# A two-block trunk kernel on one core: the second block's branch mix made from high and low fp32r parts, its weights in jobs of 128 columns, and the gate z moved ahead of the attention

## The chip, the cores and the metric

The kernel runs on one core of one Trainium2 chip. The metric is the device time of one execution in microseconds (us). Times of the kernel before: 4222.12, 4228.13 and 4229.13 us in three runs, median 4228.13 us.

## The reference, cut to what matters

Two transformer-like blocks follow one another on 1024 tokens of width 1024, all in float32. The change is in the second block, between its attention and its output projection:

```
h  = rms_norm(x, g_norm1) * (1 + sc1) + sh1           # 1024 tokens x 1024
hc = the same for 256 context tokens
aq, ak, av, dq, dk, dv, dz, da, db, ga, gd = split_cols(h @ w_in)
y_attn = window_ctx_attention(q_a, k_a, v_a, k_ac, v_ac, sink)      # 1024 x 512
o_dl   = gated delta rule over dq, dk, dv (both directions)         # 1024 x 512
y_d = rms_norm(o_dl, dn_norm_g) * silu(dz)                          # "gate z"
y   = sigmoid(ga) * (y_attn @ w_br_attn) + sigmoid(gd) * (y_d @ w_br_dn)   # branch mix
x   = x + gt1 * (y @ w_out)
x   = x + gt2 * mlp(x)                                              # 1024 -> 4096 -> 1024
```

`ga` and `gd` are 1024 wide, `w_br_attn` and `w_br_dn` are 512 x 1024. The branch mix is therefore two passes (attention, then delta rule) over 1024 x 1024 results, each result with a gate product of depth 1024 and a branch product of depth 512.

## The kernel before, in words

Every engine has an instruction stream of its own, written out by hand as a list of calls (`tensor`, `vector`, `scalar`, `gpsimd`, `sync`), and semaphores order them. Eight PSUM tiles of 128 x 512 are handed out in a ring by `Banks`: `open` takes the next one, `vacant` waits until the one eight places earlier has been emptied, `full` waits for a filled one. So an engine that empties a tile late holds TensorE up only when the ring comes round to that tile.

The stages of the second block, in TensorE's order, are: the delta rule; `qkv2` (queries, keys and values of the attention); `row` (the gain gt1 spread over the partitions); `watt`, the attention; `gated`, which makes y_d; `mix` with ps = 2 (attention branch) and ps = 3 (delta branch); `proj`, the output projection; and `ff`, the MLP.

`watt` runs over 64 units (8 query blocks x 8 heads). In its turn i TensorE makes the scores of unit i (L2281, local keys and context keys), turns the probabilities of unit i-3 (L2290) and multiplies those of unit i-4 with the values (L95). VectorE takes the scores out of PSUM (L2318, L2322), finds the maximum (L2325, L2327), makes the reciprocal for unit i-1 (L2333, L2335), and on every second turn copies a finished result out of PSUM (L2341, `tensor_copy` into `aq`). ScalarE makes the exponentials (L2352, L2353) and copies the turned probabilities of unit i-3 out of PSUM (L2362). GpSimd scales the probabilities (L2372). Scores live in 3 buffers, probabilities in 5, turned ones in 4.

`gated` makes z for 8 token tiles; for each, ScalarE a tanh, VectorE four operations (L2438 to L2446), and TensorE turns the result (L2397); ScalarE copies it to `yd` (L2413).

`mix` runs over 16 halves in a pass: 8 groups of 128 output columns, each for two halves of 512 tokens. A half has a gate product of 8 matmuls (tile "mg") and a branch product of 4 (tile "mo"), all float32, 128x128 weights by 128x512 tokens. ScalarE takes the tanh of "mg" (L837), VectorE multiplies with "mo" (L867), and in the second pass GpSimd adds the two branches (L896). The weights come as strips of 512 or 1024 columns, 2 MB each, into four fixed slots; SyncE issues each strip once a named product is through with the slot. The same functions serve the first block (ps = 0 and 1), which the change leaves as it is.

`ff` is written the other way. Each float32 operand is split into a high part that is rounded to fp32r, and a low part, the rest: ScalarE copies the weights to the high part (L1030), VectorE subtracts for the low part (L1037); activations likewise (L1099 and L1144). A product is then three fp32r matmuls: low x high, high x low, high x high. The weights of one job are 1 MB.

The normed tokens h of the second block lie in `HT`, are written to DRAM (`h_stash`) during the delta rule and read back before `qkv2`.

Of the kernel before, what the change touches and what calls it, by code (L numbers as in the profile page):

```python
# [130 lines left out]
def build(nc, d, out):  # L131
    ctx = ExitStack()
    with ctx:
# [12 lines left out]
        with nc.sbuf_tensor("below1", [P, 43008], F32), nc.sbuf_tensor("raw1", [P, 2048], F32) as RAW1, \  # L146
                nc.sbuf_tensor("between", [P, 3072], F32), nc.sbuf_tensor("turned", [P, 512], F32) as TMN:
            pass
        RR = ctx.enter_context(nc.sbuf_tensor("halves", [P, 52480], F32R))
# [53 lines left out]
        def strip_there(name):  # L203
            slot = STRIPS[name][0]
            k = 1 + [m for m in STRIPS if STRIPS[m][0] == slot].index(name)
            return l_w[slot].at(k + (1 if slot == BRA_SLOT and k >= BRA_NTH else 0))

# [25 lines left out]
            "bra": (0, None, 4, 1024, ("qkv", 7)),  # L233
            "g2a0": (1, w2[:, 2848:3360], 8, 512, ("kvv", 9)),
            "g2a1": (2, w2[:, 3360:3872], 8, 512, ("z", 7)),
            "brd": (3, d["w_br_dn_2"], 4, 1024, ("wp", 62)),
            "g2d0": (1, w2[:, 3872:4384], 8, 512, ("mg", 2, 0, 3, 1)),
            "g2d1": (2, w2[:, 4384:4896], 8, 512, ("mg", 2, 1, 3, 1)),
            "w20": (0, d["w_out_2"][:, 0:512], 8, 512, ("mo", 2, 1, 3, 1)),
            "w21": (3, d["w_out_2"][:, 512:1024], 8, 512, ("mo", 3, 1, 3, 1)),  # L240
        }
        BRA_SLOT = 0
        BRA_NTH = 1 + [m for m in STRIPS if STRIPS[m][0] == BRA_SLOT].index("bra")

        def sync_strip(e, name):
            slot, src, kt, n, after = STRIPS[name]
            if after is not None:
                e.wait_ge(*bk.full(after))
            view = strip_view(name)
            if name == "bra":  # L250
                for half in range(2):
                    e.dma_start(view[64 * half:64 * half + 64, :, :],
                                d["w_br_attn_2"][256 * half:256 * half + 256, :].rearrange(
                                    "(j f) n -> f j n", f=64)).then_inc(*l_w[slot].tick())
            else:
                e.dma_start(view, src.rearrange("(k p) n -> p k n", p=P)).then_inc(*l_w[slot].tick())
# [159 lines left out]
        def tensor_tm(e, st, key, t, N, emptied, c0=0):  # L416
# [5 lines left out]
            chain(e, o[:, 0:N], [(hlhs(k, t), w[:, k, c0:c0 + N]) for k in range(8)]).then_inc(*bk.filling(key))  # L422
# [318 lines left out]
        def vector_rec(e):  # L741
# [13 lines left out]
            for t in range(8):  # L755
# [22 lines left out]
        tmpy = [R(CB + i * 512, 512) for i in range(4)]  # L778
# [7 lines left out]
        yd = R3(F1, 4, 1024)  # L786
# [3 lines left out]
               (("ro0", "ro1"), ("gr0", "gr1"), 8, lambda k, n0, N: RC[:, k, n0:n0 + N], HB2, False),  # L790
               (("bra", "bra"), ("g2a0", "g2a1"), 4, lambda k, n0, N: aq[:, k, n0:n0 + N], None, True),
               (("brd", "brd"), ("g2d0", "g2d1"), 4, lambda k, n0, N: yd[:, k, n0:n0 + N], None, True)]
# [105 lines left out]

        o_ev, o_ad = C("proj_emptied_dve"), C("proj_added")
        G1 = R(CB + 2048, 1024)  # L900
# [19 lines left out]
        def vector_proj_tile(e, blk, c, t):  # L920
            key = ("wo", blk, c, t)
            dst = X[:, t, c * 512:(c + 1) * 512]
            i = c * 8 + t
            e.wait_ge(*bk.full(key))
            if blk == 0:
                e.scalar_tensor_tensor(out=dst, in0=bk.tile(key)[:, :], scalar=0.5, in1=dst, op0=ALU.mult,
                                       op1=ALU.add).then_inc(*bk.emptying(key))
            else:
                if i >= 4:
                    e.wait_ge(*o_ad.at(i - 3))  # L930
                elif i == 3:
                    e.wait_ge(*x_ad.at(32))
                e.scalar_tensor_tensor(out=tmpy[i % 4], in0=bk.tile(key)[:, :], scalar=0.5,
                                       in1=G1[:, c * 512:c * 512 + 512], op0=ALU.mult,
                                       op1=ALU.mult).then_inc(*bk.emptying(key))
# [32 lines left out]
        def gpsimd_proj(e):  # L968
            for c in range(2):
                for t in range(8):  # L970
                    dst = X[:, t, c * 512:(c + 1) * 512]
                    e.wait_ge(*bk.clear(("wo", 1, c, t)))
                    e.tensor_tensor(dst, dst, tmpy[(c * 8 + t) % 4], ALU.add).then_inc(*o_ad.tick())
# [577 lines left out]
        UNSPILL = [(0, 256), (256, 640), (640, 1280)]  # L1551
# [588 lines left out]
        wn = R(F0 + 8320, 384)  # L2140
        sk = R(F0 + 8704, 8)
# [9 lines left out]
        def tensor_qkv2(e):  # L2151
            for i in range(10 + 2):
                if i < 10:
                    for c0 in (c0 for c0, c1 in UNSPILL if c0 // 128 == i):
                        e.wait_ge(*l_unspill[c0].at(1))
                    if i < 8:
                        tensor_tm(e, "aq", ("qkv", i), i, 512, k_ea)
                    tensor_tm(e, "akv", ("kvv", i), i, 256, k_ea)
# [95 lines left out]
        sc_ = [R(T1 + i * 640, 640) for i in range(3)]  # L2254
        pp_ = [R(T1 + 1920 + i * 640, 640) for i in range(5)]
        pT_ = [R3(T1 + 5120 + i * 640, 5, 128) for i in range(4)]
# [49 lines left out]

        def vector_watt(e):
            e.wait_ge(*l_wn.at(1))
            e.wait_ge(*l_sk.at(1))
            for i in range(64 + 4):  # L2310
# [26 lines left out]
                if 0 <= u < 64 and u % 2:  # L2337
# [3 lines left out]
                    e.tensor_copy(aq[:, j, n * 128:(n + 1) * 128], bk.tile(key)[:, 0:128]).then_inc(*bk.emptying(key))  # L2341

        def scalar_watt(e):
            for i in range(64 + 3):
# [11 lines left out]
                if 0 <= u < 64:  # L2356
                    if u >= 4:
                        e.wait_ge(*bk.full(("wp", (u - 4) - (u - 4) % 2)))
                    for c0, n4 in watt_quads(u):
# [4 lines left out]
                                     ACT.Copy).then_inc(*bk.emptying(key))  # L2364

# [19 lines left out]
        def tensor_gated(e):  # L2385
            for i in range(9):
                if i < 8:
                    tensor_tm(e, "z", ("z", i), i, 512, y_ev)
# [87 lines left out]
        l_x2, l_x3, l_out = LD("x2"), LD("x3"), LD("out")  # L2476
        x_of = lambda src: src.rearrange("(t p) n -> p t n", p=P)

        def tensor(e):
# [18 lines left out]
            tensor_row(e, 0, TM1)  # L2498
            tensor_watt(e)
            tensor_gated(e)  # L2500
            for ps in (2, 3):
                if ps == 2:
                    e.wait_ge(*bk.clear(("wp", 62)))
                else:
                    e.wait_ge(*bk.clear(("zt", 7)))
                tensor_mix(e, ps)
# [3 lines left out]
        def vector(e):  # L2510
# [27 lines left out]
            vector_row(e, 16, TM1)  # L2538
            vector_watt(e)
            vector_gated(e)  # L2540
            vector_mix(e, 2)
            vector_mix(e, 3)
# [4 lines left out]
        def scalar(e):  # L2547
# [21 lines left out]
            scalar_gated_root(e)  # L2569
            scalar_watt(e)  # L2570
            scalar_gated(e)
            scalar_mix(e, 2)
            scalar_mix(e, 3)
# [3 lines left out]
        def gpsimd(e):  # L2577
# [16 lines left out]
            e.wait_ge(*y_z.at(8))  # L2594
            gpsimd_mix(e, 3)
            e.wait_ge(*l_x3.at(1))
# [3 lines left out]
        def sync(e):  # L2600
# [47 lines left out]
            for c0, c1 in UNSPILL:  # L2648
                if c0:
                    e.wait_ge(*e_o.at(16))  # L2650
                e.dma_start(HT[:, :, c0:c1], h3[:, :, c0:c1]).then_inc(*l_unspill[c0].tick())
# [103 lines left out]
```

## Time and profile before

| what | value |
| --- | --- |
| median of the runs | 4228.13 us (4222.12 to 4229.13) |
| the profiled execution | 4222.77 us, of which the profile's span is 4220.9 us |
| mean granted TensorE clock | 0.969 of full speed |
| TensorE busy (PE) | 4017.8 us, 95% of the span |
| VectorE (DVE) / ScalarE (ACT) / GpSimd (POOL) busy | 1733.0 / 1014.7 / 691.2 us |
| DMA | 211.36 MB, mean 50 GB/s |

PE is TensorE's matmul, PEld its weight load, which overlaps it. Times in the trace are counted from the start of the span. A float32 matmul stands in the trace as two records. Some matmul records are missing from the trace, so the period of the work is better read from the engine that empties PSUM than from a count of matmuls.

### The profile page before, as it was taken

To read this page: it belongs to the slowest core of one execution; us is meant where nothing else is said; L and a number is where in the kernel's file an instruction comes from. 1 tells how busy PE (TensorE), PEld (TensorE's weight loads), DVE (VectorE), ACT (ScalarE), POOL (GpSimd) and SP (SyncE) were. 2 spreads that over 40 slices of the span, in tenths; PEclk is the share of its full clock that TensorE was granted. 3 is DMA by queue.
4 is the path that set the end of the run, shared out by engine and by line. 5 is a ranking of instruction groups with operands and counts; after the bars stand their busy time and mean duration, and the time that the engine had idled before them with its cause. 6 is when DMAs were issued, how large, how long until landed. Compare 5 with 4: busy or idle time off the path is not lost. (4 is left out here: it accounts for less than half of the span.)

```text
span 4220.9 us, 41996 instructions
## 1 busy us (share of the span) xinstructions
PE 4017.8 (95%) x16528; PEld 2670.7 (63%) x16528; DVE 1733.0 (41%) x3083; ACT 1014.7 (24%) x1757; POOL 691.2 (16%) x533
## 2 busy tenths in 40 slices
PE   8988999999999999999988998979999998999998
PEld 4465444444468888887546888657544447888886
DVE  2165776532132332234557895477300023322232
ACT  1044553000032112213433322145200012112210
POOL 1053000000001001101011110035100112333333
PEclk9999999999999999998998997989999999999999
DMA  3200102333011111122002121210102001111111
GB/s 143 58 1 3 44 4 70 110 110 130 30 40 50 50 50 50 49 78 113 1 5 42 30 41 43 96 37 1 40 20 80 8 23 60 50 50 40 50 50 50
DMA packets 179089, 211.36 MB, mean 50 GB/s; under 512 B 63952, under 2 KB 125008, under 8 KB 178512
## 3 DMA queue, kind: packets, MB, share of 16 engines
q1 hardware_dynamic: 119536, 172.50, 12.2%
q10 hardware_dynamic: 59360, 36.19, 3.2%
q8 instruction: 134, 2.20, 0.2%
q14 instruction: 59, 0.48, 0.0%
HBM read 185.33 MB, written 21.50 MB: 49 GB/s over the span
## 5 line engine op out<-in xcount | busy, mean ns | idle before, releaser
L95 PE MATMUL ps<-arena 128*128 128x512 f32 (+4 forms) x5360 | 1915.1, 514 | 53.1 <-DVE arena L550 25.2
L95 PEld LDWEIGHTS ps<-arena 128*128 128x128 f32 (+1 forms) x5360 | 934.6, 189 | 970.1 <-issue 911.3
L95 PE MATMUL ps<-halves 128*128 128x512 f32 x6144 | 1401.4, 390 | 20.9 <-DVE halves L388 11.0
L95 PEld LDWEIGHTS ps<-halves 128*128 128x128 f32 x6144 | 1157.0, 188 | 263.9 <-DVE halves L388 11.2
L1144 DVE TENSOR_TENSOR halves<-tmps,halves 128x512 fp32r<-128x512 f32 x128 | 88.6, 692 | 524.0 <-ACT halves L1099 524.0
L1123 POOL TENSOR_TENSOR tmps<-tmps 128x512 f32<-128x512 f32 x128 | 137.4, 1074 | 999.8 <-ACT tmps L1091 999.8
L867 DVE SCALAR_TENSOR_TENSOR arena<-arena,ps 128x512 f32<-128x512 f32 x64 | 43.8, 686 | 507.4 <-PE ps L95 507.3
L1030 ACT ACTIVATE halves<-raws 128x2048 fp32r<-128x2048 f32 x62 | 118.4, 1910 | 555.5 <-PE ps L95 524.6
L896 POOL TENSOR_TENSOR arena<-arena 128x512 f32<-128x512 f32 x32 | 41.5, 1297 | 1067.2 <-DVE arena L867 1067.2
L1130 POOL TENSOR_TENSOR arena<-arena 128x512 f32<-128x512 f32 x128 | 164.6, 1293 | 191.5 <-DVE arena L1167 191.5
L1037 DVE TENSOR_TENSOR halves<-raws,halves 128x2048 fp32r<-128x2048 f32 x62 | 142.1, 2292 | 73.6 <-ACT halves L1030 73.6
L1167 DVE TENSOR_TENSOR arena<-ps,arena 128x512 f32<-128x512 f32 x128 | 87.8, 690 | 194.9 <-PE ps L95 188.7
L1091 ACT ACTIVATE tmps<-ps 128x512 f32<-128x512 f32 x128 | 76.5, 598 | 376.6 <-PE ps L95 376.6
L1159 DVE TENSOR_TENSOR arena<-arena,ps 128x512 f32<-128x512 f32 x128 | 87.2, 686 | 187.8 <-PE ps L95 187.8
L574 POOL TENSOR_SCALAR arena<-arena,sm 128x512 f32<-128x512 f32 x64 | 100.0, 1562 | 238.2 <-DVE sm L543 238.2
L1649 POOL TENSOR_TENSOR arena<-arena 128x512 f32<-128x512 f32 x40 | 49.5, 1261 | 512.1 <-PE ps L95 261.3
L2372 POOL TENSOR_SCALAR arena<-arena,wst 128x640 f32<-128x640 f32 (+1 forms) x64 | 115.3, 1803 | 104.5 <-DVE wst L2335 104.5
L886 DVE SCALAR_TENSOR_TENSOR arena<-arena,sc 128x256 f32<-128x256 f32 x224 | 117.4, 524 | 8.0
L1099 ACT ACTIVATE halves<-tmps 128x512 fp32r<-128x512 f32 x128 | 81.1, 634 | 149.2 <-POOL tmps L1123 149.2
L837 ACT ACTIVATE arena<-ps,hb 128x512 f32<-128x512 f32 x32 | 21.9, 686 | 387.4 <-PE ps L95 387.4
L1755 DVE TENSOR_TENSOR arena<-arena 64x30 f32<-64x30 f32 (+5 forms) x300 | 102.0, 340 | 13.2 <-ACT arena L1453 3.2
L1758 DVE TENSOR_TENSOR arena<-arena 64x30 f32<-64x30 f32 (+5 forms) x300 | 102.1, 340 | 10.3
(262 smaller groups left out, 3218.5 us busy)
## 6 DMA issues: line engine op xcount, KB each, us to landing
arena<-in_w_in SPq DMA_DIRECT2D x20, 2048.0 KB, 8.6
raws<-in_w_ff SPq DMA_DIRECT2D x31, 1024.0 KB, 5.4
raws<-in_w_mlp SPq DMA_DIRECT2D x31, 1024.0 KB, 5.2
arena<-in_w_ada ACTq DMA_DIRECT2D x24, 1024.0 KB, 5.2
arena<-in_w_out SPq DMA_DIRECT2D x4, 2048.0 KB, 13.8
h_stash<-arena SPq DMA_DIRECT2D x1, 5120.0 KB, 21.3
inverses<-arena ACTq DMA_DIRECT2D x20, 256.0 KB, 2.9
arena<-in_x SPq DMA_DIRECT2D x4, 1024.0 KB, 10.6
```

The lines of the kernel that those rows point to most:

```text
L95: ins = e.matmul(out_ap, l, r, start=i == 0, stop=i == n - 1)
L574: e.tensor_scalar(pbuf[i % 4], pbuf[i % 4], c[:, 2:3], None, ALU.mult).then_inc(*a_sl.tick())
L886: e.scalar_tensor_tensor(out=a, in0=raw_a[:, kk, :], scalar=sc3[:, kk, b:b + 1], in1=a, op0=ALU.mult, op1=ALU.add).then_inc(*(m_part if kk ...
L1030: e.activation(RR[:, FW + q * 4096:FW + q * 4096 + 2048], raw_of(n), ACT.Copy).then_inc(*f_wh.tick())
L1037: e.tensor_tensor(RR[:, FW + q * 4096 + 2048:FW + q * 4096 + 4096], raw_of(n), RR[:, FW + q * 4096:FW + q * 4096 + 2048].bitcast(F32), ALU ...
L1123: e.tensor_tensor(tt, tt, tt, ALU.mult).then_inc(*f_sq.tick())
L1130: e.tensor_tensor(dst, dst, tmg[(i * 8 + t) % 2], ALU.add).then_inc(*f_ad.tick())
L1144: e.tensor_tensor(fl[:, m, n0:n0 + N], ftmp[x % 2], fh[:, m, n0:n0 + N].bitcast(F32), ALU.subtract).then_inc(*f_fl.tick())
L1167: e.tensor_tensor(tmg[x % 2], bk.tile(key)[:, :], G2[:, nh * 512:nh * 512 + 512], ALU.mult).then_inc(*bk.emptying(key))
L1755: e.tensor_tensor(T3, bc(W3[:, k:k + 1, k + 1:32], [64, k, 31 - k]), bc(W3[:, 0:k, k:k + 1], [64, k, 31 - k]), ALU.mult).then_inc(*dv.tick())
L1758: e.tensor_tensor(W3[:, 0:k, k + 1:32], W3[:, 0:k, k + 1:32], T3, ALU.add).then_inc(*(i_sol if k == 30 else dv).tick())
L2372: e.tensor_scalar(p[:, 0:nl + 256], p[:, 0:nl + 256], wst[:, i % 8, 3:4], None, ALU.mult).then_inc(*w_sl.tick())
```

## The change

1. `mix` for ps = 2, 3 is replaced by `mix2`. Each product of depth 8 or 4 is three fp32r matmuls per depth step, as in `ff`. The weights of one group of 128 columns (8 gate and 4 branch tiles, 768 KB) are one job; 16 jobs, two raw buffers. ScalarE rounds the 128x1536 weights to the high part, VectorE subtracts for the low part.
2. The tokens are split into high and low parts during `watt`: at turns 6, 9, ..., 51 ScalarE makes a 128x512 high part and VectorE, at the end of the same turn, the low part (16 pieces). The attention's result is split as it leaves PSUM: the copy writes the high part, and a second VectorE instruction, behind a wait for the first, the low part (32 of them).
3. y_d is split during the first pass of `mix2` (8 pieces of 128x512).
4. `gated` comes ahead of `watt` on TensorE, VectorE and ScalarE.
5. The tokens are read back into other buffers (`HT2`, `HC`) in seven transfers, where there were three; x is read back in two halves, one during the second pass and one after it; and the projection's first strip is loaded when job 14 is through, its second at the end of the mix.

```diff
+        def sync_mix2(e, j):
+            ps, c, m = JOBS2[j]
+            c0 = c * 512 + m * 128
+            if j >= 2:
+                e.wait_ge(*bk.full(("mo",) + JOBS2[j - 2] + (1,)))
+            else:
+                e.wait_ge(*bk.full(("kvv", 9)))
...
+            e.dma_start(raw[:, 0:8, :], w2[:, g0:g0 + 128].rearrange("(k p) n -> p k n", p=P)).then_inc(*ld.tick())
...
+        def scalar_mix2_weights(e, j):
...
+            e.wait_ge(*weights2_there(j))
+            if j >= 2:
+                e.wait_ge(*bk.full(("mo",) + JOBS2[j - 2] + (1,)))
+            e.activation(RR[:, o + 1536:o + 3072], MW2[j % 2][:, :], ACT.Copy).then_inc(*m2_hi.tick())
+        def vector_mix2_weights(e, j):
...
+            e.wait_ge(*m2_hi.at(j + 1))
+            e.tensor_tensor(RR[:, o:o + 1536], MW2[j % 2][:, :], RR[:, o + 1536:o + 3072].bitcast(F32),
+                            ALU.subtract).then_inc(*m2_lo.tick())
+        def three(e, o, lefts, rights):
+            prods = []
+            for (lh, ll), (rh, rl) in zip(lefts, rights):
+                prods += [(ll, rh), (lh, rl), (lh, rh)]
+            return chain(e, o, prods)
+        def tensor_mix2(e, ps):
+            for i, (c, m, h) in enumerate(MIXED):
...
+                key = ("mg", ps, c, m, h)
+                o = bk.open(key, x_ea)
+                e.wait_ge(*bk.vacant(key))
+                e.wait_ge(*m2_lo.at(j + 1))
+                if j == 0:
+                    e.wait_ge(*h_lo.at(8 * (h + 1)))
+                three(e, o[:, :], W[0:8], [(H2H[k][:, n0:n0 + 512], H2L[k][:, n0:n0 + 512]) for k in range(8)]
+                      ).then_inc(*bk.filling(key))
...
+        def scalar_mix2(e, ps):
+            for i, (c, m, h) in enumerate(MIXED):
+                u = (ps % 2) * 16 + i
+                if h == 0:
+                    scalar_mix2_weights(e, (ps - 2) * 8 + i // 2 + 1)
...
+        def vector_mix2(e, ps):
+            for i, (c, m, h) in enumerate(MIXED):
...
+                if h == 0:
+                    vector_mix2_weights(e, (ps - 2) * 8 + i // 2 + 1)
...
-        UNSPILL = [(0, 256), (256, 640), (640, 1280)]
+        UNSPILL = [(0, 256), (256, 640), (640, 1024), (1024, 1280)]
...
+        SPLIT_AT = {6 + 3 * x: (x % 8, x // 8) for x in range(16)}
+        def scalar_tokens_hi(e, kk, h):
...
+            e.activation(H2H[kk][:, cols], HT2[kk // 4][:, kk % 4, cols], ACT.Copy).then_inc(*h_hi.tick())
+        def vector_tokens_lo(e, kk, h):
...
+            e.wait_ge(*h_hi.at(h_lo.n + 1))
+            e.tensor_tensor(H2L[kk][:, cols], HT2[kk // 4][:, kk % 4, cols], H2H[kk][:, cols].bitcast(F32),
+                            ALU.subtract).then_inc(*h_lo.tick())
...
@@ vector_watt, every second turn, and at the end of the turns in SPLIT_AT
-                    e.tensor_copy(aq[:, j, n * 128:(n + 1) * 128], bk.tile(key)[:, 0:128]).then_inc(*bk.emptying(key))
+                    e.tensor_copy(AQH[:, j, cols], bk.tile(key)[:, 0:128]).then_inc(*dv.tick())
+                    e.wait_ge(*dv.now())
+                    e.tensor_tensor(AQL[:, j, cols], bk.tile(key)[:, 0:128], AQH[:, j, cols].bitcast(F32),
+                                    ALU.subtract).then_inc(*bk.emptying(key))
+                if i in SPLIT_AT:
+                    vector_tokens_lo(e, *SPLIT_AT[i])
@@ scalar_watt, at the end of the turn, behind the copies of unit i-3
+                if i in SPLIT_AT:
+                    scalar_tokens_hi(e, *SPLIT_AT[i])
@@ the order on TensorE (VectorE and ScalarE likewise)
             tensor_row(e, 0, TM1)
+            tensor_gated(e)
             tensor_watt(e)
-            tensor_gated(e)
             for ps in (2, 3):
-                if ps == 2:
-                    e.wait_ge(*bk.clear(("wp", 62)))
-                else:
-                    e.wait_ge(*bk.clear(("zt", 7)))
-                tensor_mix(e, ps)
+                tensor_mix2(e, ps)
@@ the order on VectorE, behind vector_watt
+            vector_mix2_weights(e, 0)
+            vector_mix2(e, 2)
+            vector_mix2(e, 3)
@@ the SyncE queue
-            for st in ("bra", "g2a0", "brd", "g2a1", "g2d0", "g2d1"):
-                sync_strip(e, st)
-            e.wait_ge(*bk.full(("mo", 2, 1, 3, 1)))
-            e.wait_ge(*l_stash.at(1))
-            e.dma_start(X, x_of(xs)).then_inc(*l_x3.tick())
-            for st in ("w20", "w21"):
-                sync_strip(e, st)
+            for j in range(16):
+                sync_mix2(e, j)
+                if j == 10:
+                    e.wait_ge(*l_stash.at(1))
+                    e.dma_start(X[:, 0:4, :], x_of(xs)[:, 0:4, :]).then_inc(*l_x3[0].tick())
+            sync_strip(e, "w20")
+            e.wait_ge(*bk.full(("mo", 3, 1, 3, 1)))
+            e.dma_start(X[:, 4:8, :], x_of(xs)[:, 4:8, :]).then_inc(*l_x3[1].tick())
+            sync_strip(e, "w21")
```

## Rows read from the trace of the kernel before

**Rows 1.** The page's first part: busy time, share of the span, instructions.
```profile
PE 4017.8 (95%) x16528; PEld 2670.7 (63%) x16528; DVE 1733.0 (41%) x3083; ACT 1014.7 (24%) x1757; POOL 691.2 (16%) x533
```

**Rows 2.** Windows over attention, mix, MLP: length, busy by engine, granted clock, DMA.
```profile
2776.00:2978.00 202.00, 196.93 (x1155) 139.82 (x1154) 143.03 (x415) 109.18 (x307) 115.34 (x64) 0.97 0.00 1
...
3041.70:3379.70 338.00, 338.00 (x785) 149.37 (x785) 21.95 (x32) 19.70 (x33) 20.20 (x16) 0.99 0.11 40
...
3526.00:4150.00 624.00, 624.00 (x2753) 516.49 (x2752) 182.52 (x200) 127.00 (x148) 207.06 (x171) 1.00 0.15 48
```

**Rows 3.** Timeline of ScalarE in the mix: start, us, engine, line, idle before.
```profile
3060.58 0.60 ACT L837 ACTIVATE arena<-ps 128x512 f32<-128x512 f32 x1 [9.70 <-PE ps L95]
3070.88 0.60 ACT L837 ACTIVATE arena<-ps 128x512 f32<-128x512 f32 x1 [9.70 <-PE ps L95]
```

**Rows 4.** Timeline of ScalarE in the MLP, one entry for each 24 fp32r matmuls.
```profile
3799.06 0.60 ACT L1091 ACTIVATE tmps<-ps 128x512 f32<-128x512 f32 x1 [3.06 <-PE ps L95]
...
3804.50 0.60 ACT L1091 ACTIVATE tmps<-ps 128x512 f32<-128x512 f32 x1 [3.06 <-PE ps L95]
```

**Rows 5.** The page's groups by line: the splitting instructions of the MLP.
```profile
L1144 DVE TENSOR_TENSOR halves<-tmps,halves 128x512 fp32r<-128x512 f32 x128 | 88.6, 692 | 524.0 <-ACT halves L1099 524.0
...
L1030 ACT ACTIVATE halves<-raws 128x2048 fp32r<-128x2048 f32 x62 | 118.4, 1910 | 555.5 <-PE ps L95 524.6
...
L1037 DVE TENSOR_TENSOR halves<-raws,halves 128x2048 fp32r<-128x2048 f32 x62 | 142.1, 2292 | 73.6 <-ACT halves L1030 73.6
...
L1099 ACT ACTIVATE halves<-tmps 128x512 fp32r<-128x512 f32 x128 | 81.1, 634 | 149.2 <-POOL tmps L1123 149.2
```

**Rows 6.** Timeline of one turn of the attention and the start of the next.
```profile
2900.19 0.56 DVE L2318 SCALAR_TENSOR_TENSOR arena<-ps,arena 128x384 f32<-128x384 f32 x1 [0.55 <-PE ps L2281]
...
2901.97 0.21 DVE L2327 TENSOR_SCALAR wst<-wst,arena 128x1 f32<-128x1 f32 x1
...
2902.22 0.29 ACT L2352 ACTIVATE wst<-arena,wst 128x1 f32<-128x1 f32 x1 [1.45 <-DVE wst L2327]
2902.28 0.16 DVE L2335 RECIPROCAL wst<-wst 128x1 f32<-128x1 f32 x1
2902.42 0.81 ACT L2353 ACTIVATE arena<-arena,wst 128x640 f32<-128x640 f32 x1
...
2902.45 1.34 PE L2281 MATMUL ps<-arena 64*128 64x384 f32 x4
2902.54 1.88 POOL L2372 TENSOR_SCALAR arena<-arena,wst 128x640 f32<-128x640 f32 x1 [1.32 <-DVE wst L2335]
...
2903.23 0.74 ACT L2362 ACTIVATE arena<-ps 128x512 f32<-128x512 f32 x2
2903.39 0.56 DVE L2318 SCALAR_TENSOR_TENSOR arena<-ps,arena 128x384 f32<-128x384 f32 x1 [0.95 <-PE ps L2281]
...
2903.72 0.76 PE L2290 MATMUL ps<-identm,arena 128*128 128x128 f32 x5
...
2905.76 0.29 DVE L2341 COPY arena<-ps 128x128 f32<-128x128 f32 x1
```

**Rows 7.** Timeline: the attention's last instructions, and the last of the gate.
```profile
2977.87 0.60 ACT L2362 ACTIVATE arena<-ps 128x512 f32<-128x512 f32 x1 [1.01 <-PE ps L2290]
...
2979.65 0.29 DVE L2341 COPY arena<-ps 128x128 f32<-128x128 f32 x1 [2.13 <-PE ps L95]
...
3041.72 0.60 ACT L2413 ACTIVATE arena<-ps 128x512 f32<-128x512 f32 x1 [3.22 <-PE ps L2397]
```

**Rows 8.** DMA issues of the whole span: KB each, median us to landing.
```profile
raws<-in_w_mlp SPq DMA_DIRECT2D x31, 1024.0 KB, 5.2
...
arena<-in_w_out SPq DMA_DIRECT2D x4, 2048.0 KB, 13.8
```

**Rows 9.** Timeline of the projection: one VectorE and one GpSimd instruction that overlap.
```profile
3428.56 2.28 DVE L1037 TENSOR_TENSOR halves<-raws,halves 128x2048 fp32r<-128x2048 f32 x1
...
3428.72 3.24 POOL L973 TENSOR_TENSOR arena<-arena 128x512 f32<-128x512 f32 x1 [5.61 <-DVE arena L933]
```

More of the change, by code:

```diff
@@ L205, in strip_there @@
             k = 1 + [m for m in STRIPS if STRIPS[m][0] == slot].index(name)
-            return l_w[slot].at(k + (1 if slot == BRA_SLOT and k >= BRA_NTH else 0))
+            return l_w[slot].at(k)
         SLOTS = [W0, W0 + 4096, W0 + 8192, F0 + 12288]
@@ L249, in sync_strip @@
             view = strip_view(name)
[L250 to L254, printed above, removed]
-            else:
-                e.dma_start(view, src.rearrange("(k p) n -> p k n", p=P)).then_inc(*l_w[slot].tick())
+            e.dma_start(view, src.rearrange("(k p) n -> p k n", p=P)).then_inc(*l_w[slot].tick())
         hrhs = lambda k, n0, N: HT[:, k, n0:n0 + N]
@@ L421, in tensor_tm @@
             e.wait_ge(*strip_there(st))
-            chain(e, o[:, 0:N], [(hlhs(k, t), w[:, k, c0:c0 + N]) for k in range(8)]).then_inc(*bk.filling(key))
+            chain(e, o[:, 0:N], [(tokens(k, t), w[:, k, c0:c0 + N]) for k in range(8)]).then_inc(*bk.filling(key))
         def tensor_qkv(e):
@@ new lines, in build, with weights2_there, weights2 @@
+        l_m = [LD("mix_weights0"), LD("mix_weights1")]
+        m2_hi, m2_lo = C("mix_weights_hi"), C("mix_weights_lo")
+        yd_hi, yd_lo = C("gated_hi"), C("gated_lo")
+        parts2 = lambda j: 3 if j < 8 else 2
+        def weights2_there(j):
+            return l_m[j % 2].at(sum(parts2(x) for x in range(j % 2, j + 1, 2)))
+        def weights2(j, part, k):
+            o = PL2[j % 2] + (1536 if part == "hi" else 0) + k * 128
+            return RR[:, o:o + 128]
+        YDH = [RR[:, o:o + 512] for o in [26624 + 512 * i for i in range(5)] + [37376 + 512 * i for i in range(3)]]
@@ new lines, in three @@
+        def three(e, o, lefts, rights):
[5 more added lines that the diff above has]
+            for i, (c, m, h) in enumerate(MIXED):
+                j = (ps - 2) * 8 + i // 2
+                n0 = h * 512
+                W = [(weights2(j, "hi", k), weights2(j, "lo", k)) for k in range(12)]
+                key = ("mg", ps, c, m, h)
[6 more added lines that the diff above has]
+                      ).then_inc(*bk.filling(key))
+                key = ("mo", ps, c, m, h)
+                o = bk.open(key, x_ev)
+                e.wait_ge(*bk.vacant(key))
+                if ps == 2:
+                    e.wait_ge(*bk.clear(("wp", 62)))
+                    right = [(AQH[:, k, n0:n0 + 512], AQL[:, k, n0:n0 + 512]) for k in range(4)]
+                else:
+                    e.wait_ge(*yd_lo.at(8))
+                    right = [(YDH[2 * k + h], YDL[2 * k + h]) for k in range(4)]
+                three(e, o[:, :], W[8:12], right).then_inc(*bk.filling(key))
@@ L2473, in build @@
         TM1, TM2 = R3(Z2 + 1024, 8, 128), R3(47104, 8, 128)
[L2476 removed]
+        l_x2, l_out = LD("x2"), LD("out")
         x_of = lambda src: src.rearrange("(t p) n -> p t n", p=P)
```

134 lines of the change are left out of this document (94 added, 40 removed).

## The prediction

> **What bounds the kernel now.** I read the page first: TensorE is busy for 95% of the span, every other engine for less than half of it [rows 1]. So time is won or lost where TensorE's own work gets shorter or where it is made to wait. Then the windows of the stages that the change touches [rows 2]. In the mix TensorE is busy for all of the 338 us, while VectorE, ScalarE and GpSimd work about 20 us each: that stage is TensorE's work and nothing else, and its neighbours have room. In the attention TensorE is busy for 197 of 202 us, but here VectorE has 143 us of work, ScalarE 109 and GpSimd 115; the room is small, and what is added lands in a chain. The MLP, already written in high and low parts, keeps TensorE busy for all of its 624 us at a granted clock of 1.00, that is 2.4 GHz, so the new form can be fed. Last I read the timelines for periods.
>
> **The products.** In the mix ScalarE's tanh comes once per half, 3060.58 and then 3070.88: 10.30 us for 12 float32 products of 128x128 by 128x512 [rows 3], 0.86 us each. In the MLP one relu follows another at 3799.06 and 3804.50: 5.44 us for 24 fp32r matmuls [rows 4], 0.227 us each. A half of the new mix has 12 x 3 = 36 of these, 8.16 us. There are 32 halves: 32 x (10.30 - 8.16) = **68.5 us less**. The price of one matmul is well known, since shapes and operand types are those of the MLP, so this term has an error of about 1 us.
>
> **The weights.** A job is two halves, 16.3 us. Its split costs ScalarE 1910 ns x 1536/2048 = 1.43 us and VectorE 2292 ns x 1536/2048 = 1.72 us [rows 5]. The load for job j+1 is issued when job j begins. It must land, be rounded and be subtracted before job j+1: 16.3 - 1.43 - 1.72 - about 0.2 for semaphores leaves 12.9 us for the transfer. The trace has no transfer of 768 KB in rows of 512 bytes. By bytes, a 1024 KB load lands in 5.2 us [rows 8], which makes 3.9 us; by rows (this load has 1536 of 512 bytes, the other 1024 of 1 KB) 7.8 us. The longer end still leaves 5 us, so I take nothing. While ScalarE waits for the load it holds up the tanh, and VectorE behind it the multiply, but the ring of eight tiles covers two jobs. The y_d pieces (0.63 and 0.69 us each, eight times) go into halves of 8.16 us: nothing. The first projection strip is 2 MB, asked for 16.3 us before the projection, and lands in 13.8 us [rows 8]: nothing, with 2 us to spare. x and the second strip are needed some 30 and 55 us into the projection: nothing.
>
> **The attention.** This is where a cost falls. A turn takes 3.20 us (2900.19 to 2903.39), and VectorE's own part ends at 2902.44; it then sits idle 0.95 us until the next scores are there [rows 6]. So it could do a turn in 2.2 us. Two things are added.
> The second instruction at the copy out of PSUM: 0.29 us for the copy [rows 6], as much again for the subtraction and some 0.1 us of waiting between, 0.65 us together with the copy, on every second turn.
> The token pieces, on every third turn. VectorE's low part stands at the end of its turn, and waits for ScalarE's high part of the same turn, which stands behind ScalarE's exponentials and its copies. In the times of rows 6: the maximum is out at 2902.18, ScalarE's exponentials run until 2903.23, its two copies until 2903.97, the high part (0.63, rows 5) until 2904.60, then VectorE's low part (0.69) until 2905.35 [rows 5, 6]. Such a turn is 5.15 us long for VectorE, 2.2 of it spent waiting, with the next unit's scores, maximum and reciprocal queued behind it. It must make that good in the two following turns. Over six turns (two with pieces, four without, three copies of which one hides in a wait): 2 x 5.15 + 4 x 2.2 + 2 x 0.65 = 20.4 us. TensorE needs 6 x 3.20 = 19.2 us. VectorE becomes the bound by 1.2 us per six turns, 7.5 times between turns 9 and 53: 9 us. The PSUM ring adds a little: the tile that the subtraction frees is wanted again within the next turn of TensorE, and following the turns with this rule gives 1.6 in place of 1.2, that is 12 us. I take **10 us more**. Below, it could be nothing, if ScalarE reaches its copies earlier than drawn and the three score buffers smooth the rest; above, see the rivals.
>
> **The port.** GpSimd's scaling begins at 2902.54, right behind the reciprocal, and ends at 2904.42 [rows 6]; the low part would begin at 2904.65, so by the rows they miss one another by 0.2 us. That they would disturb one another is seen elsewhere: an addition of GpSimd that began 0.16 us into a VectorE subtraction with two SBUF inputs took 3.24 us where its neighbours take 1.26 [rows 9]. The Trainium skill's page "SBUF — State Buffer", section "Who interferes with whom", states this as a rule: a VectorE instruction with two SBUF inputs and a GpSimd instruction that reads SBUF share a read port, and the later one waits for the whole of the other. The trace agrees, in that one addition. By the rows' order the sum stays at 10 us for the attention; by the rule, were the 16 low parts each to meet a scaling, it would be the rival with the port below.
>
> **The seam behind the attention.** Before, the gate's first product starts at once. Now TensorE's first mix product waits for the weights of job 0, which VectorE splits after its last attention instruction. ScalarE's last copy ends at 2978.47, the rounding at 2979.90. VectorE's last copy runs from 2979.65 to 2979.94 [rows 7], its new subtraction ends at 2980.3, the weights' low part 1.72 us later, at 2982.0. TensorE is done at 2979.6. It waits 2.5 us and a semaphore: **2.6 us more**, between 1 and 4.
>
> **The gate moved.** The same instructions run in another place. Its last turn costs TensorE the same wait, 3.22 us in the trace [rows 7], since ScalarE and VectorE must finish tile 7 before it can be turned. Its strip and its row of gains are loaded long before. VectorE's sums of squares and the row product still come first on their queues. I take nothing. The one thing that can differ is TensorE's clock at the attention's start. The attention's window has a mean granted clock of 0.97 against 1.00 in the MLP [rows 2]: 3% of 202 us, 6 us, is all that a low clock costs there. It could go (6 us less) or double (6 us more); the idle stretches that bring it are the same, so zero.
>
> **The sum.** -68.5 + 10 + 2.6 = -55.9 us. The profiled execution took 4222.77 us, its span and 1.9 us around it; it would become 4166.9. The median of the runs lies 5.4 us above that execution, so the median forecast is 4228.1 - 55.9 = **4172 us**.
>
> **Rivals.**
> *The attention isn't slowed.* For it: the average load of VectorE stays under 3.2 us per turn if the wait for ScalarE were not there, and three score buffers give slack. Against it: VectorE is the engine that waits, and a wait of 2.2 us is longer than the 0.95 us it has spare. Then 68.5 - 2.6 = 65.9 us less: 4162.
> *The port.* For it: the gap of 0.2 us is small, and when VectorE runs late the phases move. Against it: the scaling is released by VectorE's own reciprocal, which always stands just ahead of the wait. If each of the 16 low parts waited for one scaling of 1.88 us [rows 6], 30 us come on top: 4202. Half of it gives 4187. A TensorE that idles more and is granted a lower clock goes the same way.
> *The weights come late: slower than before.* One mechanism: the load of a job in rows of 512 bytes, at the start of each job's period. If landing takes L, a period is L + 1.43 + 1.72 + 0.2, and 15 periods follow the first job. All of the gain is gone when 16.3 + 15 x period = 329.6 - 12.6, at a period of 20.05 us, that is L = 16.7 us. At L = 20 the mix takes 367 us and the kernel 4278. The nearest rows say 5.2 us for a larger load [rows 8], three times less than needed. A slower end for the first strip (13.8 us) is also under it.
>
> **How the numbers follow.** The forecast has 0.60, with a range of its own of 4164 to 4184. The attention not slowed 0.18. The port, or any other loss of over 15 us in the attention, 0.18. The late weights 0.03, and 0.01 for a no-change by a mixture. 0.2% is 8.5 us, about what a measurement of this kernel can tell from no change; all cases but the last two are beyond it on the fast side: faster 0.96, same 0.01, slower 0.03. The range goes from 4158 (the unslowed attention with a few us of clock won back) to 4190 (half of the port's price): it leaves out about 0.15, most of it above.
>
> **What the profile after would show.** The tanh of the mix every 8.16 us, TensorE busy throughout the mix, VectorE some 50 us of work in it. If the tanh is at more, the products or the weights are the failed step; waits of TensorE for VectorE's weight subtraction, once a job, would name the weights. In the attention: VectorE idle for some 2 us ahead of each of 16 subtractions, released by ScalarE; TensorE idle ahead of its scores or transposes, released by VectorE; the stage some 10 us longer than 202. If GpSimd's scaling or the subtraction has a maximum far above 1.88 and 0.69 us, it is the port. Behind the attention one TensorE wait of 2.6 us. The gate some 62 us long, with one wait of 3.2 us. The forecast is wrong above all if the attention's growth is not 10 us; next, if the transfers take over 13 us.

## The result, and the profile after

| | before | changed |
| --- | --- | --- |
| median of 4 runs | 4226.39 us (4222.12 to 4229.13) | 4190.49 us (4187.09 to 4196.68) |
| span of the profiled execution | 4220.9 us | 4185.3 us |
| mean granted TensorE clock | 0.969 | 0.964 |

The ratio is 0.9918, 95% interval 0.99 to 0.9935: faster by 36 us. The forecast was 56 us less, 4172, with a range of 4158 to 4190, so the direction was right, the size was not, and the time lies just outside the range.

The mix first. ScalarE's timeline, changed kernel:

```profile
3237.09 0.60 ACT L998 ACTIVATE arena<-ps 128x512 f32<-128x512 f32 x1 [6.65 <-PE ps L95]
3244.76 1.49 ACT L942 ACTIVATE halves<-mixw 128x1536 fp32r<-128x1536 f32 x1 [7.08 <-DMA mixw<-in_w_br_dn]
3246.16 0.58 ACT L998 ACTIVATE arena<-ps 128x512 f32<-128x512 f32 x1
3253.41 0.60 ACT L998 ACTIVATE arena<-ps 128x512 f32<-128x512 f32 x1 [6.67 <-PE ps L95]
```

The tanh of a job's second half comes at 3237.09 and 3253.41, 16.32 us apart: 8.16 for a half, where it was 10.30 [rows 3]. The tanh of the first half is late, since ScalarE stands 7.08 us for the weights' transfer; that costs nothing. The windows of the attention (its first scores to its last product) and of the mix:

```profile
2839.26:3073.91 234.65, 215.14 (x1169) 151.78 (x1168) 160.31 (x462) 118.10 (x322) 115.50 (x64) 0.91 0.00 1
...
3076.30:3337.30 261.00, 260.97 (x1151) 216.21 (x1152) 51.39 (x54) 42.54 (x54) 19.38 (x15) 1.00 0.21 59
```

TensorE is busy throughout the mix. The attention is the surprise. In the kernel before, the same stretch was:

```profile
2775.50:2979.60 204.10, 199.03 (x1170) 141.71 (x1169) 143.03 (x415) 110.00 (x307) 115.34 (x64) 0.97 0.00 1
```

It grew by 30.6 us, where 10 were forecast. TensorE's idle time in it went from 5.1 to 19.5 us, and its busy time, with the same matmuls, from 199.0 to 215.1, at a granted clock of 0.91 in place of 0.97.

The whole difference of the spans, from the stages' ends in both timelines (each to some 0.2 us, by the instruction taken as the end): everything up to the gate +1.3; the gate +0.3; the attention +30.6; the seam behind it +2.4; the mix -69.9; all behind it -0.3. Together -35.6 us.

One late turn in the timeline of the changed kernel (weight loads and GpSimd left out):

```profile
2923.76 0.21 DVE L2464 TENSOR_SCALAR wst<-wst,arena 128x1 f32<-128x1 f32 x1
...
2924.21 0.81 ACT L2496 ACTIVATE arena<-arena,wst 128x640 f32<-128x640 f32 x1
...
2925.02 0.74 ACT L2505 ACTIVATE arena<-ps 128x512 f32<-128x512 f32 x2
...
2925.66 0.62 ACT L2436 ACTIVATE halves<-tokens 128x512 fp32r<-128x512 f32 x1
...
2926.31 0.69 DVE L2441 TENSOR_TENSOR halves<-tokens,halves 128x512 fp32r<-128x512 f32 x1 [2.07 <-ACT halves L2436]
2926.92 0.55 DVE L2455 SCALAR_TENSOR_TENSOR arena<-ps,arena 128x384 f32<-128x384 f32 x1
...
2928.70 0.21 DVE L2464 TENSOR_SCALAR wst<-wst,arena 128x1 f32<-128x1 f32 x1
...
2929.14 0.81 ACT L2496 ACTIVATE arena<-arena,wst 128x640 f32<-128x640 f32 x1
...
2929.74 0.33 PE L2413 MATMUL ps<-identm,arena 128*128 128x128 f32 x1 [0.37 <-DVE halves L2481]
...
2929.96 0.74 ACT L2505 ACTIVATE arena<-ps 128x512 f32<-128x512 f32 x2
...
2930.84 2.15 PE L95 MATMUL ps<-arena 128*64 128x128 f32 x10 [0.77 <-ACT arena L2505]
```

VectorE waits 2.07 us for ScalarE's high part, where 2.2 were forecast. Its next maximum is out 4.94 us after the last one (2923.76 to 2928.70), so ScalarE's next exponentials and, behind them, its copies of turned probabilities are late, and TensorE's product with the values waits for those copies, 0.77 us here. Just before, TensorE's last transpose also waited 0.37 us for the second instruction at the copy (L2481), which holds a tile of the ring. Up to the attention's last turns the first of these waits is the large one, by the view of TensorE's waits (us in total, times, longest); the kernel before has none of either there:

```profile
PE ps L95 <- ACT arena L2505: 12.2, 12, 1.6
PE ps L2413 <- DVE halves L2481: 2.6, 7, 0.4
```

After the waits of this turn the granted clock falls; windows of 5 us:

```profile
2926.00:2931.00 5.00, 3.85 (x24) 2.52 (x23) 4.52 (x12) 2.03 (x6) 1.96 (x2) 1.00 0.00 0
2931.00:2936.00 5.00, 5.00 (x17) 3.41 (x16) 1.85 (x7) 1.75 (x5) 2.04 (x2) 0.51 0.02 5
```

0.51 is the lower level, 1.2 GHz. There are five such falls in the middle of the attention; the kernel before has a low clock at the attention's start, and none later. At the lower level TensorE takes longer for a turn, and behind four of the five falls it doesn't wait when VectorE is late the next time: of VectorE's 16 late turns it waits for 12, 14.8 us in all.

### The profile page after: what moved, and what is told of

The parts are those of the page before. It is cut to its first block and busy times, and to the rows that moved or that the text cites. A ratio compares the mean times of both kernels' runs of the same rounds, so it can differ in the third digit from the quotient of the medians.

```text
span 4185.3 us, 42926 instructions
## 1 busy us (share of the span) xinstructions
PE 3963.6 (95%) x16912; PEld 2751.7 (66%) x16912; DVE 1783.1 (43%) x3155; ACT 1049.6 (25%) x1797; POOL 692.6 (17%) x533
## 5 line engine op out<-in xcount | busy, mean ns | idle before, releaser
L95 PE MATMUL ps<-halves 128*128 128x512 f32 x7296 | 1665.0, 391 | 23.3 <-DVE halves L378 11.0
L95 PEld LDWEIGHTS ps<-halves 128*128 128x128 f32 x7296 | 1374.7, 189 | 312.2 <-issue 11.4
L95 PE MATMUL ps<-arena 128*128 128x512 f32 (+4 forms) x4208 | 1448.2, 501 | 65.2 <-DVE arena L544 25.0
L95 PEld LDWEIGHTS ps<-arena 128*128 128x128 f32 (+1 forms) x4208 | 721.9, 190 | 736.2 <-issue 667.4
L95 PE MATMUL ps<-arena,tokens 128*128 128x512 f32 (+1 forms) x384 | 140.0, 522 | 0.0
L830 ACT ACTIVATE arena<-ps,hb 128x512 f32<-128x512 f32 x32 | 21.9, 686 | 389.9 <-PE ps L95 389.9
L95 PEld LDWEIGHTS ps<-arena,tokens 128*128 128x128 f32 x384 | 72.3, 191 | 62.1 <-issue 59.1
L860 DVE SCALAR_TENSOR_TENSOR arena<-arena,ps 128x512 f32<-128x512 f32 x32 | 21.9, 687 | 202.4 <-PE ps L95 202.4
```

Source lines behind the costliest of these rows:

```text
L95: ins = e.matmul(out_ap, l, r, start=i == 0, stop=i == n - 1)
```

## The experiments

Three theories. **A, the wait:** VectorE's wait for ScalarE makes it late, and TensorE has no lead to absorb it. **B, the work:** VectorE's added instructions, or their meeting with GpSimd at a shared port. **C, the ring:** the second instruction at the copy out of PSUM. The attention's length is read for each as above, from the first scores to the last product with the values.

**1. The low part one turn later.** In `vector_watt`:

```diff
-                if i in SPLIT_AT:
-                    vector_tokens_lo(e, *SPLIT_AT[i])
+                if i - 1 in SPLIT_AT:
+                    vector_tokens_lo(e, *SPLIT_AT[i - 1])
```

> The low part of each token piece is made by VectorE at the end of the turn after the one in which ScalarE makes its high part; nothing else is changed. Theory A (the wait: VectorE stands 1.4 to 2.1 us in its own turn for ScalarE's high part, and TensorE has only some 0.3 us of lead, so the lateness passes on to it): the wait is gone, the attention falls from 234.6 us to between 205 and 212 (before: 204.1), its granted clock from 0.91 back to 0.97, and the kernel lands near 4160 to 4167. Theory B (VectorE's added work of 17 us itself, or the port that it shares with GpSimd): the attention stays at 228 us or more. Theory C (the second instruction at the copy out of PSUM, which holds a tile of the ring): it stays at 228 or more.

Measured: the attention 207.6 us; the kernel 4160.64 us, ratio to the kernel before 0.9852 (0.982 to 0.9885). Theory A's number; B and C fall.

**2. The high part first.** In `scalar_watt`, the same work on both engines, in the same turn:

```diff
+                    if i in SPLIT_AT:
+                        scalar_tokens_hi(e, *SPLIT_AT[i])
                     e.wait_ge(*w_mx.at(i + 1))
...
-                if i in SPLIT_AT:
-                    scalar_tokens_hi(e, *SPLIT_AT[i])
```

> ScalarE makes the high part of a token piece at the start of its turn, ahead of the exponentials, while it waits for the maximum anyway; VectorE's low part stays at the end of the same turn. VectorE then begins it right behind its reciprocal, just as GpSimd begins to scale. Theory A: no wait of VectorE for ScalarE ahead of the low part, the attention at 205 to 213 us. Theory B, by the port: the low part or the scaling next to it takes 0.6 to 1.9 us longer in each of 16 turns, and the attention stays at 225 us or more. Theory C: 228 or more.

Measured: one run of 4159.61 us, the attention 203.3:

```profile
2842.94:3046.26 203.32, 198.26 (x1169) 141.26 (x1168) 162.00 (x462) 118.02 (x322) 118.23 (x64) 0.98 0.00 1
```

VectorE has as much work in it as in the changed kernel (162.0 against 160.3 us), and the stage is 31 us shorter. As for the port, all 16 low parts now overlap a scaling of GpSimd, and they do so in two orders, eight times each:

```profile
2975.41 0.67 DVE L2441 TENSOR_TENSOR halves<-tokens,halves 128x512 fp32r<-128x512 f32 x1
2975.59 2.25 POOL L2517 TENSOR_SCALAR arena<-arena,wst 128x640 f32<-128x640 f32 x1 [1.32 <-DVE wst L2472]
...
2985.20 1.88 POOL L2517 TENSOR_SCALAR arena<-arena,wst 128x640 f32<-128x640 f32 x1 [1.32 <-DVE wst L2472]
2985.74 0.79 DVE L2441 TENSOR_TENSOR halves<-tokens,halves 128x512 fp32r<-128x512 f32 x1
```

Alone, as in the changed kernel, the low part takes 0.69 us and the scaling 1.88. Where the low part begins 0.18 us ahead, the scaling takes some 0.36 us longer; where it begins 0.34 to 0.55 us behind, the low part takes 0.79 us (once 1.00), and the scaling nothing more. No low part waits for a whole scaling. What is left of it on the path is at most the 0.5 us by which this attention is longer than that of run 4 below.

**3. Without the second instruction at the copy.** The branch product of the first pass takes the high part twice; the low part of the attention's result is left out of the computation.

```diff
-                    e.tensor_copy(AQH[:, j, cols], bk.tile(key)[:, 0:128]).then_inc(*dv.tick())
-                    e.wait_ge(*dv.now())
-                    e.tensor_tensor(AQL[:, j, cols], bk.tile(key)[:, 0:128], AQH[:, j, cols].bitcast(F32),
-                                    ALU.subtract).then_inc(*bk.emptying(key))
+                    e.tensor_copy(AQH[:, j, cols], bk.tile(key)[:, 0:128]).then_inc(*bk.emptying(key))
```

> The second VectorE instruction at the copy out of PSUM is left out, and the branch product of the first pass uses the high part in its place (the low part of the attention's result is left out of the computation). Theory A: the attention falls only by what 32 instructions of 0.3 us take from the catching up, to between 225 and 234 us, and the waits for ScalarE stay. Theory C: the attention falls to 215 us or less.

Measured: one run of 4190.39 us, the attention 232.7. C falls: TensorE's 2.6 us of waits for L2481 are gone, and those for ScalarE's copies take their place, 15.7 us in place of 12.2.

**4. All pieces behind the attention.**

```diff
             vector_watt(e)
+            for x in SPLIT_AT.values():
+                vector_tokens_lo(e, *x)
             vector_mix2_weights(e, 0)
```

(and ScalarE's high parts likewise; none inside.)

> All 16 token pieces are split behind the attention, so none is in it. Theories A and B: the attention at 205 to 208 us, and TensorE waits behind it for 16 low parts and the weights, some 13 us in place of 2.4; the kernel near 4170. Theory C: the attention stays at 225 us or more, since the second instruction at the copy is still in it. Beside e1 it tells A from B: if e1 is as fast in the attention as e4, the work of the 16 low parts costs nothing there and only the wait did.

Measured: one run of 4172.99 us, the attention 202.8, TensorE's wait behind it 12.05. Beside run 2 with its 203.3: sixteen low parts in the attention cost 0.5 us there, once nothing waits. The work is nearly free, and the wait was the price.

**5. The seam.** As run 2, with the weights of job 0 rounded in turn 60 and subtracted in turn 64.

```diff
+                if i == 60:
+                    scalar_mix2_weights(e, 0)
                 u = i - 3
...
                     e.reciprocal(c[:, 3:4], c[:, 1:2]).then_inc(*w_rc.tick())
+                if i == 64:
+                    vector_mix2_weights(e, 0)
```

> As the run with the high part first, and the weights of job 0 are rounded by ScalarE in turn 60 of the attention and subtracted by VectorE in turn 64, where it waits for TensorE anyway. Theory A with the seam as costed: the attention stays at 203 us, TensorE's wait of 2.4 us behind it goes, the kernel some 2 us faster than the one with the high part first: near 4157, about 0.983 to 0.985 of the kernel before. If the wait stays at 2.4 us, something else than the weights releases the first mix product.

Measured: 4159.26 us (4154.75 to 4165.43), ratio 0.9846 (0.983 to 0.9862). TensorE's wait behind the attention, 2.42 us in the changed kernel and in run 2, is gone: the product begins as the attention ends. The attention was 209.3 us here, against 203.3: not by waits, its idle time is 6.9 us, but by its start, where the clock stayed low some 9 us longer. The kernel's time doesn't show the 2 us.

**6. Half of the waits.** As run 2, but at even turns the high part stays at the end of the turn.

> Pieces at odd turns have their high part first, pieces at even turns keep it at the end of the turn, so VectorE waits in 8 turns in place of 16. Theory A: the cost goes with the number of waits, the attention at some 219 us (half way between 203 and 235). If the granted clock falls only when idle stretches follow one another closely, it stays at 0.97 and the attention is at 212 to 216, since the idle part alone is 14 us for 16 waits.

```profile
2846.47:3061.07 214.60, 200.31 (x1169) 141.65 (x1168) 160.40 (x462) 118.08 (x322) 115.50 (x64) 0.98 0.00 1
```

Measured: one run of 4176.48 us, the attention 214.6, at a clock of 0.98. Eight waits cost (214.6 - 203.3) / 8 = 1.4 us each, 1.15 of it idle time (14.3 against 5.1 us in all), and the clock didn't fall in the middle. Sixteen at this price make 22.6 us, 225.9; the changed kernel has 234.7. The other 9 us are what its falls of the clock cost on balance: its busy time is 16 us above the kernel before, but a slower TensorE waits less. So the cost has two parts. With half of the waits the second didn't come; what brings it is not shown.

**7 and 8. VectorE late by work.** As run 2, with one or three more subtractions per piece into unused places.

```diff
             e.wait_ge(*h_hi.at(h_lo.n + 1))
+            for r in range(1):   # 3 in the second
+                e.tensor_tensor(RR[:, (3072, 3584, 7168)[r]:(3584, 4096, 7680)[r]], HT2[kk // 4][:, kk % 4, cols],
+                                H2H[kk][:, cols].bitcast(F32), ALU.subtract).then_inc(*dv.tick())
+            e.wait_ge(*dv.now())
```

> High part first, and VectorE does one more subtraction of the same size per piece, into an unused place (16 more of 0.69 us; the result is not used). VectorE's part of such a turn grows from 2.9 to 3.6 us, or 4.2 with the copy, against TensorE's 3.2 and its lead of 0.3. Theory A (what counts is VectorE's lateness beyond that lead, whatever its reason): 0.1 us in half of the turns and 0.7 in the others, the attention at 207 to 212 us. If TensorE could run ahead by a turn or more, as the forecast had it, the two following turns would take it up and the attention would stay at 203 to 205.

> As the last, with three more subtractions per piece: VectorE's part of such a turn is some 5.0 us, near the 5.15 us of the change, but filled with work and with no wait for ScalarE. Theory A: as late, so as slow: the attention at 228 to 240 us, and the granted clock near 0.91. If it is ScalarE's wait itself that matters and not VectorE's lateness, the attention stays below 220.

Measured: one more, 4171.84 us and an attention of 216.5; three more, 4221.81 us and 271.0, at clocks of 0.96 and 0.78:

```profile
2842.05:3058.56 216.51, 203.02 (x1169) 143.87 (x1168) 174.14 (x478) 118.11 (x322) 118.41 (x64) 0.96 0.00 1
```

```profile
2837.30:3108.30 271.00, 249.99 (x1169) 176.05 (x1168) 196.46 (x510) 118.09 (x322) 122.54 (x64) 0.78 0.00 1
```

Both are above what was expected. With one more, the idle time grew by 8.4 us (13.5 against 5.1), where lateness beyond the lead was expected to cost 8 x 0.1 + 8 x 0.7 = 6.4; the other 4.8 us are busy time, from a low clock at the start. With three more VectorE is as late as in the changed kernel or a little later, since the copy out of PSUM no longer hides in a wait and GpSimd's scaling runs beside the subtractions (up to 2.77 us where it takes 1.88). Idle time is 21.0 us, close to the changed kernel's 19.5. But TensorE's busy time is 250.0 us in place of 215.1, all by the clock. That lateness by work costs what lateness by waiting costs holds for the idle part; how far the clock falls was not foreseen.

**9. TensorE's idle stretches filled.** As run 5, with three float32 matmuls each ahead of the last gate tile and of the first transposes; their results are overwritten.

```diff
+                        if u == 0:
+                            for _ in range(3):
+                                e.matmul(o[:, :], ak[:, 0:128], ak[:, 0:512], start=True, stop=True)
                         e.wait_ge(*w_sl.at(u + 1))
```

> As the run with the high part first and the weights of job 0 early. In addition TensorE does three float32 matmuls of 128x128 by 128x512 (0.86 us each at the full clock) whose result is overwritten, at two places where it sits idle: ahead of the last gate tile (3.2 us idle) and ahead of the attention's first transposes (3.6 us idle). If the idle stretches are what brings the clock down at the attention's start, its first 16 us are no longer at 0.5 to 0.7 and the attention falls from 203 to 209 us to some 197 to 200, the kernel by 4 to 8 us. If the clock falls anyway, the fillers run at half speed and cost a few us instead.

```profile
2841.00:2846.00 5.00, 3.67 (x13) 1.66 (x11) 4.72 (x16) 2.68 (x8) 3.05 (x2) 1.00 0.00 0
2846.00:2851.00 5.00, 3.90 (x16) 2.82 (x16) 2.52 (x10) 2.96 (x8) 3.21 (x3) 0.71 0.00 2
2851.00:2856.00 5.00, 5.00 (x21) 3.62 (x20) 2.86 (x9) 2.00 (x5) 1.56 (x1) 0.61 0.01 3
```

Measured: 4154.71 us (4151.42 to 4162.62), ratio 0.9837 (0.9823 to 0.985); the attention 205.5 us. The clock stays up through the filled stretches and falls at about 2848 all the same, behind small waits (0.25 to 1.30 us) in the first turns. It stays low for 7 us, where run 5's profile has two low stretches of some 4 and 17 us. The expected 4 to 8 us aren't shown: the median is 4.6 us lower, but the interval overlaps that of run 5.

**10. TensorE given a lead.** The changed kernel with all its waits; only the product with the values, and the copy out of PSUM, come one turn later.

```diff
 tensor_watt, vector_watt
-            for i in range(64 + 4):
+            for i in range(64 + 5):
...
-                u = i - 4
+                u = i - 5
 scalar_watt
-                    if u >= 4:
-                        e.wait_ge(*bk.full(("wp", (u - 4) - (u - 4) % 2)))
+                    if u >= 5:
+                        e.wait_ge(*bk.full(("wp", (u - 5) - (u - 5) % 2)))
 five buffers of turned probabilities: pT_[u % 4] -> pT_[u % 5]
```

> The changed kernel with its waits as they are; only TensorE's product of the probabilities with the values runs one turn later (unit i-5 in turn i, five buffers of turned probabilities), and the copy out of PSUM with it. Theory A in full: what left TensorE only 0.3 us of lead is that this product waits for ScalarE's copies, which stand behind the exponentials of the newest unit. With a turn more, TensorE takes up most of VectorE's late turns, and only VectorE's own load (20.4 us in six turns by the forecast's sum, against 19.2) is left: the attention at 208 to 218 us in place of 234.6, the clock near 0.97, all 16 waits of VectorE still there. If another link holds TensorE (the ring of PSUM tiles), the attention stays at 225 us or more.

```profile
2843.11:3055.98 212.87, 203.97 (x1169) 144.18 (x1168) 158.56 (x462) 118.19 (x323) 115.34 (x64) 0.95 0.00 1
```

```profile
DVE halves L2441 <- ACT halves L2436: 26.1, 16, 2.1
```

Measured: one run of 4169.82 us, the attention 212.9. The second fence is the waits' view: all 16 waits of VectorE for ScalarE are there, 26.1 us of them, where the same view has 13, of 21.9 us, for the changed kernel. The attention is 9 us longer than before and not 31, and TensorE's waits for ScalarE's copies, 12.2 us in the changed kernel, are gone. This was the link. (VectorE's copy out of PSUM moved with the product, and its waits for that product went from 12.1 to 5.5 us; the run doesn't tell the two halves of the loop apart.)

Of the 8.8 us, 3.8 are idle time and 4.9 busy time. The clock was low somewhat longer at the start, and fell once later, for some 7 us, right behind one single wait:

```profile
2877.02 1.97 PE L95 MATMUL ps<-arena 128*64 128x128 f32 x8 [1.41 <-DVE halves L2481]
```

## Why the prediction was wrong, and where it was right

**Right: the products.** 8.16 us per half was forecast and measured. The mix gave 69.9 us, where 68.5 were forecast. The rest is of the size of what the kernel before lost at the start of its mix, where the granted clock was low (0.72 and 0.94 in the two windows of 5 us from 3040); the new mix is at 1.00 throughout.

**Right: the weights.** The transfer asked for as a job began let the rounding start 4.7 to 6.4 us later, in the median 5.0, between the two bounds of 3.9 and 7.8. The rounding took 1.49 us (1.43 forecast), the subtraction 1.76 (1.72). TensorE never waited for them within the mix.

**Right: the seam,** 2.42 us for 2.6, and run 5 shows its cause. **Right: the gate,** 0.3 us.

**Wrong: the attention, 10 us forecast, 30.6 measured.** The first steps of that part held: the wait of VectorE was forecast at 2.2 us and is up to 2.1. The low part was also forecast to miss the scaling, by 0.2 us, and does, by 0.1. The step that failed is the sum over six turns: 20.4 us of VectorE against 19.2 of TensorE, hence 9 us. It takes for granted that TensorE goes on at its own pace while VectorE is late, and that VectorE catches up in the next two turns. The text went on to follow the turns "by hand with this rule", but only with the ring of tiles; it left out that the product with the values waits for ScalarE's copies, and that these stand behind the exponentials of the newest unit, which wait for VectorE's maximum. The rows of before had it. ScalarE's copies end at 2903.97 [rows 6], and the product that needs them begins at:

```profile
2904.41 0.76 PE L95 MATMUL ps<-arena 128*64 128x128 f32 x5
```

That is a lead of 0.4 us (the expectations have 0.3), against a lateness of 2. So a wait stopped TensorE at once, for some 1.15 us of idle time (run 6), and what VectorE made good later gave nothing back. Run 10 is the proof from the other side: with a lead of one turn, such as the forecast took for granted, the attention grew by 8.8 us. That this is close to the forecast's 9 is partly luck: the 9 stood for VectorE's load alone, and of the 8.8 more than half is the clock.

**Wrong as well: the clock taken as neutral in the attention.** The forecast bounded it by the 6 us that its low clock costs at the start. Waits in the middle were not thought of as bringing it down again. Read directly, the 30.6 us are 14.4 of idle time and 16.1 of busy time with the same matmuls, which is the clock. By run 6's price for a wait without a fall, the falls cost about 9 us on balance.

**The rivals.** That the attention isn't slowed did not come; it comes with either of the orders of runs 1 and 2. The port was priced at up to 30 us and would have landed at 4187 to 4202, where the kernel did land, but for another reason: in the changed kernel the low part and the scaling miss one another (the low part's maximum is 694 ns), and in run 2, where they meet, neither loses more than 0.4 us. The rival named beside it, a TensorE that idles more and is granted a lower clock, is what happened. It had no chain of its own and no worked-out price, only a share of the 0.18 for a loss of over 15 us in the attention. The late weights did not come.

**The better version.** With the high part first (run 2), and the weights early (run 5), the kernel takes 0.9846 of the time before, against 0.9918 for the change as made: the intervals (0.983 to 0.9862, and 0.99 to 0.9935) don't overlap. The 56 us forecast for the change are there, 62 by run 2 and 67 by run 5, each against the kernel before as measured beside it, once ScalarE's 16 instructions stand ahead of its exponentials and not behind.

## What to carry to other kernels

Before a delay on an engine that isn't the bound is called absorbed, measure the bound engine's lead at every link that comes back from it: the time between the end of what releases it and the start of what it releases, in the trace before. A stage in which two engines have room on average can have a lead of 0.4 us. Where a new instruction of one engine waits for a new one of another, put the first of the two where its engine idles anyway, or the second a turn later; here that one line was worth some 30 us. And once TensorE is made to wait again and again, count the clock too, as a second cost on top of the idle time.

## What the runs showed of the hardware that was not expected

The granted clock fell in the middle of a stage in which TensorE was still busy for over 90% of the time. With 8 waits of about 1.2 us of idle time spread over the stage (run 6, 14.3 us idle in all) it never fell there; with VectorE late in 16 turns it fell five times, for several us each; in run 10, with 8.9 us idle in all, it fell once, behind a single wait of 1.41 us; with VectorE's three added subtractions the stage's mean went to 0.78, for about the same idle time as in the changed kernel (21.0 and 19.5 us). So the sum of the idle time doesn't order these cases, and what separates them was not settled.

At the attention's start the clock stays low for a time that differs between kernels which are alike there: in run 2 it was back at 1.00 after 14 us, in runs 1, 5 and 7 after 23. That is some 4 to 5 us of TensorE's busy time, and blurs comparisons of single runs by as much. Filling the two longest idle stretches (run 9) didn't prevent the fall.

Two instructions that share a port did not exclude one another wholly in every case. The Trainium skill's page "SBUF — State Buffer", section "Who interferes with whom", calls the shared ports an exclusive lock. The addition of [rows 9], begun 0.16 us into a subtraction of 2.28 us, looks like that: 3.24 us in place of 1.26. Run 2 comes near it where the low part is first: 0.49 us of it were left as the scaling began, and the scaling took 0.36 us longer. Where the scaling was first, by 0.34 to 0.55 us, the low part took 0.1 us longer, once 0.3, with 1.3 us or more of the scaling still to come. And in run 8, with some 2.2 us of subtractions left as a scaling began, it took only 0.9 us longer. In these two cases the measurement differs from the page and decides: the price was far below a whole instruction.
